# The first 128 tokens through the decoder trunk by themselves

## The reference

```
h = RMSNorm(x);  z = h @ W_in                          # W_in: 1024 x 6560
A = differential attention (4 heads), B = latent attention (8 heads), C = gated convolution of 3 taps
x += W_out( sum_i sigmoid(gate_i) * (branch_i @ W_branch_i) )
# PEER: each token picks 8 x 16 of 16384 single-neuron experts by two top-16 searches
q = RMSNorm(x) @ w_query;  scores against sub_keys;  top 16 of 16 x 16 sums per head
x += sum over the token's 128 experts e of  softmax_gate * gelu(u[e] . h) * v[e]
x += sigmoid(RMSNorm(x) @ W_pg) * (p @ W_pp)            # per-layer embedding
```

## Time and profile before

| what | value |
|---|---|
| runs | 3766.02, 3770.04, 3770.3 us |
| the profiled execution | 3774.79 us, its span 3773.0 us |
| granted TensorE clock, mean | 0.892 |
| busy | PE 2929.2 us (78%), DVE 2485.5 (66%), ACT 1487.2 (39%), POOL 1332.5 (35%) |
| transferred | 1298.53 MB, mean 344 GB/s; 1073.81 MB of it by the indirect DMAs |

### The profile page before, as it was taken

The page is one execution under the profiler, slowest core; times in us unless marked ns, Lnnn a source line. Parts: engine busy times, 40 slices in busy tenths (PEclk is TensorE's granted clock), DMA queues, the critical chain, the costliest instruction groups (busy, mean ns, idle before and its releaser), DMA issues.

```text
span 3773.0 us, 28818 instructions
## 1 busy us (share of the span) xinstructions
PE 2929.2 (78%) x8156; PEld 1487.3 (39%) x8156; DVE 2485.5 (66%) x5160; ACT 1487.2 (39%) x4001; POOL 1332.5 (35%) x1033
## 2 busy tenths in 40 slices
PE   7689848777998788767989788867998885555556
PEld 4444714534436234433436234534436331111112
DVE  1221486776667876766658876776657877777774
ACT  2230224458433343457432343458433342222222
POOL 0000033333332443434333443334333445555551
PEclk9889978989999899988999898989999896777778
DMA  4214279889998999989998999889999999999994
GB/s 151 81 67 156 102 320 379 340 364 378 393 382 347 399 411 378 383 345 405 404 374 333 410 409 368 343 348 367 390 378 363 388 403 416 422 422 421 422 421 184
DMA packets 182399, 1298.53 MB, mean 344 GB/s; under 512 B 20320, under 2 KB 21856, under 8 KB 26592
## 3 DMA queue, kind: packets, MB, share of 16 engines
q0 software_dynamic: 147456, 1073.81, 70.6%
q1 hardware_dynamic: 34784, 222.88, 15.1%
HBM read 1294.51 MB, written 2.10 MB: 344 GB/s over the span
## 4 chain that ended last, share of the span: by engine, by line
PE 46%; DMA 21%; DVE 14%; ACT 13%; issue 5%; POOL 1%; SPq 0%; DVEq 0%; ACTq 0%; POOLq 0%
DMA ring<-in_uv,experts 16%; PE ps_sum L1299 12%; PE ps_act L1361 8%; PE ps_act L1533 8%; PE ps_act L1406 8%; DVE ring L1173 5%; DMA wt<-in_weights 4%; PE ps_dve L1361 3%; PE ps_dve L1561 2%; DVE x L1182 2%; ACT L750 2%; ACT L537 2%; ACT area_e L537 2%; ACT diag L758 2%; ACT weight L752 2%
## 5 line engine op out<-in xcount | busy, mean ns | idle before, releaser
L507 POOL DMA_INDIRECT ring<-in_uv,experts x1024 | 1330.0, 1299 | 2369.1 <-PE ps_sum L1299 926.5
L1299 PE MATMUL ps_sum<-ring,diag 128*128 128x512 f32 x2132 | 1240.1, 726 | 658.1 <-ACT diag L758 650.6
L1173 DVE SCALAR_TENSOR_TENSOR ring<-ring,h_ffn 128x1024 f32<-128x1024 f32 x1024 | 1233.8, 1220 | 197.9 <-DMA ring<-in_uv,experts 192.0
L1299 PEld LDWEIGHTS ps_sum<-ring,diag 128*128 128x128 f32 x2132 | 445.0, 223 | 1333.1 <-ACT diag L758 919.2
L1182 DVE SCALAR_TENSOR_TENSOR x<-ring,weight,x 128x1024 f32<-128x1024 f32 x491 | 629.4, 1282 | 213.3 <-ACT weight L752 212.9
L750 ACT ACTIVATE dots<-dots 128x1 f32<-128x1 f32 x1024 | 205.3, 201 | 1333.3 <-DVE ring L1173 1331.7
L1406 PE MATMUL ps_act<-area_h,wt 128*128 128x256 f32 x1536 | 348.6, 386 | 2.5 <-ACT area_h L523 2.5
L1533 PE MATMUL ps_act<-wt,area_h 128*128 128x512 f32 x768 | 338.6, 596 | 10.0 <-DMA wt<-in_weights 9.8
L1361 PE MATMUL ps_act<-wt,area_h 128*128 128x512 f32 (+1 forms) x768 | 331.6, 592 | 5.2 <-ACT area_h L523 5.1
L1406 PEld LDWEIGHTS ps_act<-area_h,wt 128*128 128x128 f32 x1536 | 296.2, 194 | 54.6 <-issue 11.0
L752 ACT ACTIVATE weight<-dots,gate 128x1 f32<-128x1 f32 x1024 | 301.6, 295 | 34.1
(11 more groups left out here) (171 smaller groups left out, 2047.7 us busy)
## 6 DMA issues: line engine op xcount, KB each, us to landing
wt<-in_weights SPq DMA_DIRECT2D x192, 1024.0 KB
ring<-in_uv,experts POOLq DMA_INDIRECT x1024
wt<-in_weights SPq DMA_DIRECT2D x12, 512.0 KB
wt<-in_weights SPq DMA_DIRECT2D x4, 768.0 KB
x<-in_x SPq DMA_DIRECT2D x4, 512.0 KB, 5.0
area_y<-in_keys SPq DMA_DIRECT2D x4, 512.0 KB, 9.5
area_f<-in_keys SPq DMA_DIRECT2D x4, 512.0 KB, 10.7
area_f<-in_ffn_rows SPq DMA_DIRECT2D x4, 512.0 KB, 4.0
```

The lines of the kernel that those rows point to most:

```text
L507: pool.indirect_dma_start(ring[:, row.slot, :], None, a[f"uv{row.step // 2}"][:, :], bass.IndirectOffsetOnAxis(ap=experts[:, row.step % 2, ...
L1173: dve.scalar_tensor_tensor(u, u, 1.0, h_ffn[:, row.tile, :], ALU.mult, ALU.mult, accum_out=dots[:, row.j:row.j + 1]).then_inc(dots_ready, 1)
L1299: ins = pe.matmul(ps_sum[:, b, :], diag[:, row.pe_before % DIAGS, :], ring[:, row.slot, D + b * 512:D + (b + 1) * 512], start=row.pe_first ...
```

## The change

Steps become entries of a list `STEPS` of (pair whose embedding is due, chunk whose trunk runs, rows served). A chunk is a set of one or two token tiles. Pair 0 is split into two chunks of one tile; the other three pairs stay whole. The 256 rows of pair 0 are now served in two steps, 92 beside the trunk of tile 1 and 164 beside the trunk of the second pair. `topk` of a tile always belongs to its own chunk's step.

```diff
-STEPS = DEPTH * SEQ // HALF
+@dataclass(frozen=True)
+class Chunk:
+    number: int
+    layer: int
+    half: int
+    tiles: tuple
+    ...
+    def width(self, t):
+        return (2 * self.half + t + 1) * P
+CHUNKS = [Chunk(0, 0, 0, (0,)), Chunk(1, 0, 0, (1,)), Chunk(2, 0, 1, (0, 1)), Chunk(3, 1, 0, (0, 1)), Chunk(4, 1, 1, (0, 1))]
+PAIRS = [Chunk(d, d // 2, d % 2, (0, 1)) for d in range(2 * DEPTH)]
+STEPS = [(None, CHUNKS[0], 0), (None, CHUNKS[1], 92), (None, CHUNKS[2], 2 * ROWS - 92), (PAIRS[0], CHUNKS[3], 2 * ROWS),
+         (PAIRS[1], CHUNKS[4], 2 * ROWS), (PAIRS[2], None, 2 * ROWS), (PAIRS[3], None, 0)]
...
-    if step == 0:
-        out += choice(0, 1)
...
-        out += choice(d, 0)
-        if d:
-            out += choice(d, 1)
+        for t in d.tiles:
+            out += choice(d, t)
...
             sp.dma_start(cols[:, :, :], a["cols"]).then_inc(consts_loaded, 16)
-            for t in range(2):
-                sp.dma_start(x[:, t, :], a["x"][t]).then_inc(x_loaded[t // 2], 16)
+            sp.dma_start(x[:, 0, :], a["x"][0]).then_inc(x_loaded[0], 16)
...
+                    if d.number == 0:
+                        load(0, NT_PLE, DENSE_TILES[:4])
+                        for t in range(1, 4):
+                            sp.dma_start(x[:, t, :], a["x"][t]).then_inc(x_loaded[1 + t // 2], 16)
+                        load(0, NT_PLE + 4, DENSE_TILES[4:-HEADS])
+                    else:
+                        load(d.layer, NT_PLE, DENSE_TILES[:-HEADS])
...
                 for kh in range(2):
                     w = tile(kh).rearrange("p (k n) -> p k n", k=4)
-                    for t in range(2):
+                    for t in d.tiles:
                         for k in range(4):
...
-                        ins = pe.matmul(b[:, 0:HALF], w[:, k, c * P:(c + 1) * P], hT[:, k, :],
+                        ins = pe.matmul(b[:, d.tokens], w[:, k, c * P:(c + 1) * P], hT[:, k, d.tokens],
...
-                dve.wait_ge(dots_ready, STEP_ROWS * step)
-                dve.wait_ge(row_loaded, 16 * (step + 1))
-                for t in range(2):
+                dve.wait_ge(row_loaded, 16 * (d.number + 1))
+                for i, t in enumerate(d.tiles):
+                    former = FIRST_TILE[d.number] + i - 2
+                    if former >= 0:
+                        dve.wait_ge(dots_ready, ROWS * (former + 1))
```

More of the change, by code:

```diff
@@ L1 @@
 from contextlib import ExitStack
+from dataclasses import dataclass
 import numpy as np
@@ L59 @@
 NT_PLE, NT_DENSE = len(PLE_TILES), len(DENSE_TILES)
[L62 to L72, removed]
@@ L151, in attention @@
 def attention(kind, d, heads, between):
-    out, n, between = [], 2 * heads, list(between)
+    out, n, between = [], d.n * heads, list(between)
     for i in range(n + 3):
@@ L179, in stages_of @@
                                          ("conv_b", d, 0), ("conv_b", d, 1), ("taps", d), ("latent", d)])
-        out += [("diff_sub", d, t) for t in range(2)]
+        out += [("diff_sub", d, t) for t in d.tiles]
         out += [("mla_norm", d), ("mla_up", d), ("mla_sums", d), ("mla_qk", d), ("mla_rope", d), ("mla_turn", d)]
         out += attention("mla", d, MH, mix(d, MIX_EARLY))
-        out += [("mla_out", d, t) for t in range(2)]
+        out += [("mla_out", d, t) for t in d.tiles]
         out += mix(d, MIX_LATE)
@@ L188, in stages_of, with tiles_of @@
             out += [("scores", d, i - 1), ("rank", d, i - 1)] if i else []
-        out += choice(d, 0)
-        if d:
-            out += choice(d, 1)
+        for t in d.tiles:
+            out += choice(d, t)
     return out
 TILES_OF = {"ple_out": 3, "qkv": 2, "latent": 2, "conv_c": 1, "conv_x": 1, "conv_b": 1, "mla_up": 2,
-            "gate_b": 2, "branch_first": 1, "branch_more": 1, "out": 2, "query": 1}
+            "gate_a": 2, "gate_b": 2, "branch_first": 1, "branch_more": 1, "out": 2, "query": 1}
+def tiles_of(stage):
+    name, d = stage[0], stage[1]
+    if name in ("gate_a", "gate_b") and d.tiles[-1] != (name == "gate_b"):
+        return 0
+    return TILES_OF.get(name, 0)
 def timeline():
-    base, tile, plan, where, done, pairs = [0, 0, 0, 0], 0, [], {}, [], 0
-    for step in range(-1, STEPS + 1):
+    base, tile, plan, where, done, pairs, number = [0, 0, 0, 0], 0, [], {}, [], 0, 0
+    for pair, chunk, rows in STEPS:
         row, served, spent = [], 0, 0.0
-        stages = stages_of(step)
-        with_rows = 0 <= step < STEPS
-        whole = sum(ROWS_IN[st[0]] for st in stages) if step < STEPS - 1 else STEP_ROWS
+        stages = stages_of(pair, chunk)
+        whole = sum(ROWS_IN[st[0]] for st in stages) if chunk else rows
         for st in stages:
@@ L236, in shares @@
     by_pe, due = [], 0.0
-    for step, row, rest in PLAN:
+    for row, rest in PLAN:
         for (name, *more), at, units in row:
@@ L1041, in out @@
             def out(at, d, n):
-                for t in range(2):
-                    xs = x[:, 2 * (d % 2) + t, n * 512:(n + 1) * 512]
+                for t in d.tiles:
+                    xs = x[:, 2 * d.half + t, n * 512:(n + 1) * 512]
                     take(dve.tensor_tensor(xs, bank(), xs, ALU.add))
```

468 lines of the change are left out of this document (250 added, 218 removed).

## The result

The changed kernel takes 3864.37 us (3861.88 to 3871.55, four runs) against 3770.17 us (3766.02 to 3771.51), a ratio of 1.0258 with a 95% interval of 1.0244 to 1.0271: 94 us slower. I had forecast 3803, 33 us slower. The span of the profiled execution is 3863.0 us against 3773.0, so 90.0 us are to be found in the trace.

The account below looks back on a forecast made before the run. The kernel was taken as bound by turns: transfers, TensorE, and alternating row and trunk work. Steps 283 + 401 + 695 = 1379 us against 1346 gave 33 us slower, 3803 us by the median; range 3773 to 3835, chance 0.50.

Parts of the forecast that it names:

- A: First step, trunk of tile 0 with no rows: 283 us, bounds 270 to 300, so gathers begin 214 us earlier.
- third rival: One tile idles TensorE more, so dense matmuls run at clock 0.76; total 3862 us, chance 0.10.
- B: Second step, trunk of tile 1 with 92 rows: 401 us, bounds 385 to 425, partly bound by transfers.
- second rival: Tile 1's step is weight-bound, TensorE waiting over 40 us for `wt`: 39 us more, 3842 us, chance 0.16.
- C: Third step, trunk of the second pair with 164 rows: stages sum to 709, forecast 695 us, bounds 675 to 715.
- these waits mostly go: In the second pair's step, VectorE's 18.4 us of waits for gathers mostly vanish with lighter transfers, taking 709 to 695 us.
- first rival: Transfers were the bound and the second pair's step is relieved: 616 us there, total 3724 us; chance 0.24 in all sizes.
- 0.697 of each stage's price: In the second pair's step, each stage's cost for rows in the old second trunk is scaled by 0.697; sum 709 us.
- The base: The second pair's trunk without rows, put at 525 us: 504 of the first pair's stages and 21 for wider attention.
- From about 1346 us on nothing changes: same stages, same rows: After the second pair's step, later steps keep their lengths, so only the time to that point was forecast.
- if they don't, I have missed something: Sign to check: steps after the second pair's should last as before, 848, 869 and 657 us.
- D and E: Steps of the third and fourth pairs' trunks, expected to last as before, 848 and 869 us.

Follow-up runs that it names:

- e7: e1 with the second step's dense weight loads cut to a quarter of their columns: 3820.28 us, 1.0142 to the kernel before.
- e3: e1 with no rows beside the trunk of tile 1 and all 256 beside the second pair's: 3803.75 us, 1.0087 to the kernel before.
- e5: e1 with a plain copy in place of every row's gelu, so ScalarE changes no table for rows: 3744.37 us, 0.9936 to the kernel before.
- e15: Kernel before, with attention rows at flips all given to VectorE and those at scores and pv to TensorE: 3751.81 us, 0.9949.
- e16: Kernel before, with attention rows at flips all given to TensorE and a 0.45 share of those at scores and pv: 3827.08 us, 1.0145.
- e1: Changed kernel with the running sum that deals rows set to its earlier value (0.8333) at the fourth step: 3826.84 us, 1.0155 to the kernel before.
- e2: Kernel before with the changed kernel's running sum (0.5) set at the start of its step 1: 3804.65 us, 1.0089.
- e14: e1 with the running sum set to 0.8333 at the start of C too: 3852.56 us, 1.0224 to the kernel before.
- e17: Changed kernel with attention rows at flips given to VectorE and those at scores and pv to TensorE: 3803.11 us, 1.0089 to the kernel before.

## Why the forecast was right in sign and short in size

**A was right:** 276.8 for 283 (bounds 270 to 300). Cut as in the forecast, the three stretches in which TensorE is full took 23.6, 63.6 and 33.5 us for 22.5, 62.5 and 31.9, and no other term was off by more than 3.5. The third rival, the clock, is false, though its total of 3862 us is nearly what was measured: `mix` was granted 0.97, the stretch with the convolution 0.89, `qkv` 1.00, not 0.76. The Trainium skill (TensorE: Matmul & The Clock Gate, HAM oscillation) expects a lower clock in passes over few tokens wherever matmuls are shorter than the wait for their weights; here A's `mix` with 128 tokens was busy for 65.4 of 67.5 us, so the condition did not arise, and nothing speaks against the rule.

**B was right in its sum, 401.6 for 401, by luck, and wrong in its reason.** Its terms missed both ways: `x_norm` 18.2 us for 10.5, `qkv` to `latent` 82.1 for 91, from `mla_up` to the latent attention 31.1 for 43.6, the latent attention 41.4 for 30. I had it bound by transfers in `qkv`, convolution and `mix`. It does stand at 420 to 422 GB/s in the first two and at 380 in `mix`, and at 0.94 and 376 GB/s over all (forecast over 0.9 at 355 to 365). But with a quarter of the weights it gets only 10 us shorter (e7), so the weights' transfers were not what set its length. What did isn't shown by a run: without rows B takes 279.8 us (e3), so 119 to 122 us hang on its 92 rows; VectorE waited only 5.5 us in it for gathers, TensorE's matmuls 98.5 us for diagonals. The second rival is false too: the waits of TensorE's matmuls for `wt` in B are these four, 10.6 us together (those of its weight loads are 16.3, in part the same time), where over 40 were needed:

```profile
PE ps_act L1593 <- DMA wt<-in_weights: 7.0, 3, 3.0
...
PE ps_act L1421 <- DMA wt<-in_weights: 2.5, 1, 2.5
...
PE ps_dve L1421 <- DMA wt<-in_weights: 0.7, 1, 0.7
PE ps_dve L1622 <- DMA wt<-in_weights: 0.4, 1, 0.4
```

**C failed: 721.5 for 695.** 14 of the 26.5 us are the step "these waits mostly go". They did go, and gave nothing: VectorE's 18.4 us for gathers are no longer among its waits, and in their place it waits longer for TensorE, for the scores of the latent attention (L1076, before L1020) 42.4 us for 30.8 and for the branches in `mix` (L1090, before L1034) 33.3 for 19.2. The latter cost nothing, as TensorE is busy for all of `mix`. VectorE's waits in C, the longest, and the two that answer to them before:

```profile
DVE x L1240 <- ACT weight L799: 65.5, 23, 8.8
DVE area_e L1076 <- PE ps_dve L1492: 42.4, 10, 7.3
DVE area_b L1090 <- PE ps_dve L1622: 33.3, 8, 6.6
DVE area_e L945 <- PE ps_dve L1492: 28.8, 4, 10.2
```

```profile
DVE area_e L1020 <- PE ps_dve L1432: 30.8, 13, 6.1
DVE area_b L1034 <- PE ps_dve L1561: 19.2, 7, 4.3
```

This is also the end of the first rival: transfers fell to 305 GB/s and a share of 0.81, and C is over even the 709 us of the sum without any relief. The other 12 us are the term "0.697 of each stage's price". The base was right (525 forecast, 523 bare). From `qkv` to the end of the latent attention my terms give 333.5 and the trace 349.7 (16.2 more); `query` is 5.3 over, `mix` with `out` 3.3 under, `topk` and the last ranks 6.5 under. A row's price isn't constant: the first 64 cost 1.75 us each, the next 100 some 0.9. Part of the dear first ones are table changes, which do not go by the number of rows: 89 loads for 164 rows, 90 for 256. Of C's length 28 us hang on them (e5), where 0.697 of the second trunk's 22 would be 15; so they account for about 13 us, the size of the missed term, though that the two are the same microseconds isn't shown.

**"From about 1346 us on nothing changes: same stages, same rows" failed, by 34 us.** The same stages and the same number of rows, but another deal of them to two engines, since a running sum crosses the border of a step. This was in the code, and I had said what to look for ("if they don't, I have missed something"), but had not followed what is carried over. No term and no bound of the sum covered D and E. The mechanism: TensorE works in order; a row dealt at a flip makes it wait for ScalarE's diagonal, which waits for gelu and for VectorE's `dot`, begun only then, and the flip's transposes, which the rest of the head needs next, stand behind it. e15 and e16 give all rows of the flips to VectorE or to TensorE and move the total by −16 and +59 us. That the deal costs the 34 us is shown by e1 and e2; that it is this wait rests on the traces of the differential attention. At the flips of the latent attention TensorE's rows come behind its own matmuls in any case, and still that of e16's first step is longer (120.7 us for 107.4) and those of e15 are shorter, which I did not take apart. What stays open is C: there the deal with three of five flips on TensorE (e14) is slower than that with four (135.3 us for 129.1 in e1 and 126.5 in the changed kernel, in the differential attention), so at lower density of rows something else decides; e17, with none, has 126.8.

**The change itself,** with the deal taken out, costs 57 to 61 us (e1). The points with no rows say why. Before, the bare trunks to the fourth list are 497.2 + 20 (second `topk`) + 523 = 1040 us, and 256 rows add 305. After, they are 276.8 + 279.8 + 523 = 1080, and the rows add 1399.9 − 1080 = 320. Two halves of a pair cost 39 us more than the pair, in chains that don't halve, and the rows 16 more; and starting the gathers 220 us earlier buys nothing, as a row beside B costs 1.30 to 1.86 us, no less than one beside C. So of the splits of pair 0 with the deal of before in D and E, the one with no rows in B (e3) is the least bad: 3803.75 us; e17, with 92 rows in B and the flips' rows on VectorE, takes 3803.11.

## What to carry to other kernels

When a change shifts work between steps, follow every quantity that the scheduler carries across them: here a fractional sum re-dealt the work of two untouched steps and made over a third of the loss. On an in-order engine count not only how many side jobs it takes, but what of the critical path stands behind each: give the job whose operand comes late to the place behind the critical matmuls. A wait that disappears is a gain only if the next one isn't ready to take its place, and a price per row taken from one density doesn't hold at another; a kernel with the side work left out, and one with a quarter of it, give both for two short runs.

## What the runs showed that I had not expected

Transfers at 0.94 of the time and 376 GB/s bound little: with three quarters of the weights' bytes left out, and 301 GB/s, the step was 2.5% shorter. A table load of ScalarE takes 1283 ns of the engine; the Trainium skill (ScalarE: Activation LUTs, What ACT_TABLE_LOAD costs) adds a drain of about 1.38 us, together 2.66 us for a change of set. No row here shows the drain by itself. C lost 81 of its 89 loads with gelu and got 28 us shorter, 0.35 us for each, so most of either part lay beside other work. And the first trunk, with no rows beside it and the same instructions, took from 490.6 (e2) to 497.2 us (before) in different kernels, which no run explains: differences under 7 us in one step prove nothing.
